# Gated-delta mixer of a two-layer hybrid block on one core: key and query norm sums as two float32r passes, and matrix steps dealt behind later value units

## The chip, the cores and the metric

The kernel runs on one core of a Trainium2 chip. The metric is the device time of one execution in microseconds (us); a time "of a kernel" is the median of several executions.

## The reference

The block has two layers on x of 512 tokens by 1024 features, all in float32. A layer normalises x, multiplies it by one wide matrix `w_in`, runs four mixers (a: gated delta rule, b: dilated window attention, c: stick-breaking attention, d: retention), multiplies each result by its branch matrix and a sigmoid gate, adds them, applies `w_o`, and follows with a two-matrix MLP. Cut to the part that the change touches:

```python
qkv = jax.nn.silu(causal_dwconv(gdn_qkv, conv_w))            # mixer a
qa, ka, va = split(qkv)
qa = l2norm(to_heads(qa, 4)) * 128 ** -0.5                   # x * rsqrt(sum(x*x) + 1e-6), 128 features a head
ka = l2norm(to_heads(ka, 4))
g = -exp(a_log) * softplus(gdn_a + dt_bias)                  # per token and head
oa = gated_delta_chunked(qa, ka, va, sigmoid(gdn_b), g)
#   per chunk: decay = exp(cumsum differences of g);  lower = (k*beta) k^T * decay below the diagonal
#   t_inv = (I + lower)^-1;  attn = q k^T * decay;  a scan over chunks with a 128x128 state a head
```

## The kernel before

**Engines and data.** Tensors lie feature-major: 128 features on the partitions, 512 tokens in a row. SP loads the weights in 182 units a layer of 256 rows by 512 columns; POOL splits each into a rounded float32r part (L579) and the rest (L581), in a ring of four; PE multiplies in three float32r passes, high by high, low by high, high by low (`unit`, L1744): 24 products of 512 columns for a unit of two 128-row tiles and four output tiles, so 12 for half a unit (two output tiles). The order on every engine is written out by hand in `tensor_layer`, `vector_layer`, `scalar_layer`; engines meet through counting semaphores.

**PSUM.** There are eight banks: `big0` to `big3` take the outputs of weight units, `mix0` to `mix3` everything else, in the order of the list `mixer_keys()`, each key in the next bank. A bank's next user on PE waits for `big_free`/`mix_free` of its last. The four output tiles of `av` (values) stand in big1, big2, big3, big0, and those of the next job, `gatea0`, in the same four. An `av` bank is given back by `conv_raw(i)` on ACT (i = 8 to 11): it copies the tile to a mix bank (L719) and then, scaled, to SBUF (L720), whose end frees the big bank. The mix banks of raw 8 to 11 are those of LT0, att0, LT1, att1, so `conv_raw(8)` also waits until DVE is through with LT0.

**The stage of the change (mixer a).** On PE: `aq` (queries), `ak` (keys), `aab`, then the four units of `av`. Behind them are dealt, by `value_unit(i)`:

- `l2_sums`: for each of the 4 query and 4 key head tiles, the sum of squares over the 128 partitions, as one float32 product of a matrix of ones with the squares `q_sq` (L1855);
- `gates_by_token` (four small transposes), `gc` (cumulative sums of g), `gt` (its rows);
- `decays(b)`: rows R and B of token block b, broadcast over partitions; `lower(b)` the matrix LT(b); `scores_gdn(b)` the matrix att(b).

ACT makes the squares (`qk_squares`, L731) and the roots (`qk_root`, L736, L738); DVE scales with them (`qk_normed`, L1292). After `decays`, ACT computes exponentials for blocks 0 and 1 (`row_exponents`), copies LT0 (`lower_copy`, L785), then runs `conv_raw(8)`, `conv_raw(9)`, `lower_copy(1)`, `conv_raw(10)`, `conv_raw(11)`. DVE runs for each block `beta_keys`, `lower`, `scores_out`, `first_level` (its last instruction, L1357, frees LT's bank), `first_inverse` (L1363), and only behind both blocks the convolutions 8 to 11 (`conv`, L1284 twice and L1286 each), which free the four mix banks for the products Y and X of the first level of the triangular inverse: Y of blocks 0 and 1 take the banks of raw 8 and 9, X those of raw 10 and 11. Both layers run the same program; layer 1 repeats layer 0's stage 1144.77 us later.

The order of PE in this stage is these lines (L1929 to L1946):

```python
unit(JOB["av"], 2, (0, 1)); value_unit(2); unit(JOB["av"], 2, (2, 3))
decays(0); decays(1)
unit(JOB["av"], 3, (0, 1))
lower(0); scores_gdn(0)                    # after waits for the l2 banks
unit(JOB["av"], 3, (2, 3))
lower(1); scores_gdn(1)
set_fill("gatea0", "az")                   # fills[0], fills[1]: units 0 and 1 of gatea0
for tiles in ((0, 1), (2, 3)):
    for q in range(2): unit(*fills[q], tiles)
```

Of the kernel before, what the change touches and what calls it, by code (L numbers as in the profile page):

```python
# [278 lines left out]

EIGHTHS = (("Y", 1), ("X", 1), ("Y", 2), ("Y", 3), ("Y", 4), ("X", 4), ("Y", 5), ("Y", 6))  # L280


def mixer_keys():
# [51 lines left out]
    "a_silu": 12, "a_small": 2, "a_smallact": 4, "a_sq": 8, "a_tap": 24, "a_z": 4, "a_zero": 1, "an_rs": 4,  # L335
    "an_sq": 4, "b_exp": 36, "b_fc": 3, "b_fexp": 3, "b_max": 12, "b_nm": 12, "b_ohi": 5, "b_olo": 5, "b_rhi": 9,
    "b_rlo": 9, "b_rp": 9, "b_share": 2, "b_sum": 3, "b_zinv": 1, "b_zln": 1, "big_done0": 43, "big_done1": 43,
    "big_done2": 38, "big_done3": 38, "big_free0": 43, "big_free1": 43, "big_free2": 38, "big_free3": 38,
    "c_act": 40, "c_add": 8, "c_bias": 3, "c_exp": 20, "c_half": 4, "c_hi": 8, "c_ln": 20, "c_ohi": 4, "c_pos": 20,
    "c_pv": 4, "c_pvfree": 4, "c_split": 8, "c_sum": 20, "c_z": 20, "d_nrm": 4, "d_ohi": 4, "d_olo": 4, "d_out": 4,  # L340
    "d_rope": 4, "d_rp": 4, "dn_rs": 4, "dn_sq": 4, "f_hi": 32, "f_lo": 32, "f_relu": 32, "gated_b": 8,
# [7 lines left out]
    "w_loaded3": 720, "w_ready": 182, "w_used": 182, "x_hi": 8, "x_lo": 8, "x_ss": 3, "x_ss1": 1,  # L349
# [3 lines left out]
def hybrid_kernel(nc, ins, out):  # L353
    ctx = ExitStack()
    with ctx:
# [229 lines left out]
        def scalar_layer(act, l):  # L585
# [97 lines left out]
            def gate_sigmoid(b):  # L683
                for hf in range(2):
                    if b == "c":
                        for i in range(2):
                            big_freed(act, (f"gatec{2 * hf + 1}", i))
                    else:
                        big_freed(act, (f"gate{b}{hf}", 3))
                    A(gate_at(b, hf), gate_at(b, hf), ACT.Sigmoid).then_inc(sem(f"sig{b}"), 1)  # L690
# [36 lines left out]
            def qk_squares(i):  # L727
                if i >= 4:
                    mix_wait(act, ("l2", i - 4))
                act.wait_ge(*upto("a_silu", i + 1))  # L730
                A(q_sq[:, i % 4, :], (aQ, aK)[i // 4][:, i % 4, :], ACT.Square).then_inc(sem("a_sq"), 1)  # L731
# [379 lines left out]
        def vector_layer(dve, l):  # L1111
# [87 lines left out]
            def gated_last():  # L1199

                def last_lo(k):
                    key = (f"yb{k // 4}", k % 4)
                    dve.wait_ge(*upto("m_hi", k + 1))
                    big_free(TT(hL[:, k, :], home(key)[0][:, :], f32(hH[:, k, :]), ALU.subtract), key)

                for hf in range(2):
                    for k in range(4 * hf, 4 * hf + 4):
                        ps = big_wait(dve, (f"yb{k // 4}", k % 4))
                        dve.wait_ge(*upto("sigb", k // 4 + 1))
                        TT(ps[:, :], ps[:, :], sg[:, k, :], ALU.mult).then_inc(sem("gated_b"), 1)  # L1210
                        dve.wait_ge(*upto("gated_b", k + 1))
                        TT(ps[:, :], ps[:, :], mixed[:, k, :], ALU.add).then_inc(sem("mixed_b"), 1)
                        if k % 4:
                            last_lo(k - 1)
                    last_lo(4 * hf + 3)

            def gated(b):

                for hf in range(2):
                    for i in range(4):  # L1220
                        k = 4 * hf + i
                        ps = big_wait(dve, (f"y{b}{hf}", i))
# [483 lines left out]
        def tensor_layer(pe, l):  # L1706
# [162 lines left out]
            def value_unit(i):  # L1869
                if i == 0:  # L1870
                    l2_sums(0, 1, 2, 3)
                if i == 1:
                    gates_by_token()
                    l2_sums(4, 5, 6, 7)
# [3 lines left out]
                if i == 2:  # L1878
# [539 lines left out]
```

## Time and profile before

| | |
|---|---|
| time of three runs | 2310.89, 2307.17, 2311.28 us; median 2310.89 |
| profiled execution | 2309.96 us, of it span 2308.2 us |
| PE (matmul) busy | 2282.2 us, 99% of the span |
| DVE, ACT, POOL busy | 862.5 (37%), 739.5 (32%), 1281.5 us (56%) |
| granted TensorE clock | 0.996 mean |

The profile is of one execution. "Busy" of PE is modelled, since matmuls are pipelined: a product of 512 columns is listed with 0.39 us, and the next starts 0.23 us after it. For PE's pace read the distance of starts. Start times are counted from the start of the span.

### The profile page before, as it was taken

How to read it: one execution, taken by the hardware profiler on the slowest of the kernel's cores; microseconds unless marked ns; L12 is line 12 of the kernel's file. 1: busy time of each engine (PE TensorE's matmuls, PEld its weight loads, DVE VectorE, ACT ScalarE, POOL GpSimd, SP SyncE). 2: the span in 40 equal slices, each digit the busy share in tenths (PEclk: the TensorE clock that was granted, in tenths of full speed). 3: DMA queues.
4: the chain of work that ended last, by engine and by line, in shares of the span. 5: the costliest groups of instructions: out<-in, count | busy, mean ns of one | idle time of the engine just before them, and what ended most of it. 6: DMA issues, size and time to landing. Idle time of an engine off the chain costs nothing.

```text
span 2308.2 us, 30524 instructions
## 1 busy us (share of the span) xinstructions
PE 2282.2 (99%) x12414; PEld 1848.9 (80%) x12414; DVE 862.5 (37%) x1390; ACT 739.5 (32%) x1465; POOL 1281.5 (56%) x732
## 2 busy tenths in 40 slices
PE   8999999999999999999999999999999999999998
PEld 7788877877877788888887888778778768888887
DVE  4654025424354421122355540444234545112233
ACT  5633145123044411122355340461220545102121
POOL 5523644555553566677655146546556445666874
PEclk9999999999999999999999999999999999999999
DMA  4311321423222233332223123223233123333231
GB/s 152 92 47 47 100 73 55 119 82 91 74 78 61 91 119 100 92 100 92 83 79 92 29 65 101 65 82 96 77 94 90 60 69 104 103 96 101 92 101 64
DMA packets 105899, 196.64 MB, mean 85 GB/s; under 512 B 8480, under 2 KB 18848, under 8 KB 105504
## 3 DMA queue, kind: packets, MB, share of 16 engines
q1 hardware_dynamic: 104608, 188.40, 27.1%
q10 hardware_dynamic: 1152, 6.29, 0.8%
q8 instruction: 99, 1.62, 0.3%
q14 instruction: 40, 0.33, 0.0%
HBM read 192.57 MB, written 2.10 MB: 84 GB/s over the span
## 4 chain that ended last, share of the span: by engine, by line
PE 95%; ACT 2%; DVE 2%; issue 1%; DMA 0%; DVEq 0%; ACTq 0%
PE big L1744 72%; PE mix L1744 10%; PE mix L1895 4%; PE big L2097 1%; PE mix L2065 1%; PE mix L2167 1%; PE mix L2076 1%; PE mix L1855 1%; PE mix L2295 1%; PE mix L2248 0%; PE mix L1809 0%; ACT o_hi L616 0%; PE mix L2232 0%; PE mix L2218 0%; PE mix L2024 0%
## 5 line engine op out<-in xcount | busy, mean ns | idle before, releaser
L581 POOL TENSOR_TENSOR ring_lo<-stage,ring_hi 128x1024 fp32r<-128x1024 f32 (+3 forms) x364 | 911.6, 2504 | 30.4
L579 POOL TENSOR_SCALAR ring_hi<-stage 128x1024 fp32r<-128x1024 f32 (+3 forms) x364 | 371.4, 1020 | 972.7 <-PE big L1744 892.1
L1744 PE MATMUL big<-h_hi,ring_hi 128*128 128x512 f32 (+1 forms) x1888 | 721.5, 382 | 2.9 <-DVE h_lo L1166 1.7
L1744 PE MATMUL big<-h_lo,ring_hi 128*128 128x512 f32 (+1 forms) x1888 | 708.6, 375 | 0.0
L1744 PE MATMUL big<-h_hi,ring_lo 128*128 128x512 f32 (+1 forms) x1888 | 708.5, 375 | 0.0
L1744 PEld LDWEIGHTS big<-h_hi,ring_hi 128*128 128x128 f32 x1888 | 354.7, 188 | 74.9 <-issue 8.9
L1744 PEld LDWEIGHTS big<-h_lo,ring_hi 128*128 128x128 f32 x1888 | 354.7, 188 | 66.0
L1744 PEld LDWEIGHTS big<-h_hi,ring_lo 128*128 128x128 f32 x1888 | 355.0, 188 | 62.0 <-issue 1.4
L1685 DVE TENSOR_TENSOR h_lo<-scr,h_hi 128x1024 fp32r<-128x1024 f32 x64 | 86.8, 1356 | 246.4 <-ACT h_hi L1084 246.4
L1744 PE MATMUL big<-ring_hi,h_hi 128*128 128x512 f32 x448 | 174.2, 390 | 0.0
L1744 PE MATMUL big<-ring_lo,h_hi 128*128 128x512 f32 x448 | 174.1, 390 | 0.0
L1744 PE MATMUL big<-ring_hi,h_lo 128*128 128x512 f32 x448 | 173.7, 389 | 0.0
L1084 ACT ACTIVATE h_hi<-scr 128x1024 fp32r<-128x1024 f32 x64 | 68.4, 1069 | 262.2 <-PE big L1744 260.2
L1696 DVE SCALAR_TENSOR_TENSOR scr<-big,scr 128x512 f32<-128x512 f32 x64 | 44.3, 692 | 254.5 <-ACT scr L1093 254.3
L1744 PE MATMUL mix<-ring_hi,h_hi 128*128 128x512 f32 x320 | 125.0, 391 | 0.0
L1744 PE MATMUL mix<-ring_hi,h_lo 128*128 128x512 f32 x320 | 124.6, 389 | 0.0
L1744 PE MATMUL mix<-ring_lo,h_hi 128*128 128x512 f32 x320 | 124.5, 389 | 0.0
L1093 ACT ACTIVATE scr<-big 128x512 f32<-128x512 f32 x64 | 38.3, 598 | 262.1 <-PE big L1744 261.2
L1744 PEld LDWEIGHTS big<-ring_hi,h_hi 128*128 128x128 f32 x448 | 84.1, 188 | 18.1 <-issue 0.7
L1744 PEld LDWEIGHTS big<-ring_lo,h_hi 128*128 128x128 f32 x448 | 83.8, 188 | 18.2 <-POOL ring_lo L581 1.0
L1744 PEld LDWEIGHTS big<-ring_hi,h_lo 128*128 128x128 f32 x448 | 84.1, 188 | 17.6
L1744 PE MATMUL big<-o_hi,ring_hi 128*128 128x512 f32 x224 | 90.4, 403 | 1.0 <-ACT scr L674 0.9
(302 smaller groups left out, 2717.4 us busy)
## 6 DMA issues: line engine op xcount, KB each, us to landing
stage<-in_w_in SPq DMA_DIRECT2D x168, 512.0 KB, 3.5
stage<-in_w_mlp_in SPq DMA_DIRECT2D x64, 512.0 KB, 3.6
stage<-in_w_mlp_out SPq DMA_DIRECT2D x64, 512.0 KB, 3.8
stage<-in_w_o SPq DMA_DIRECT2D x16, 512.0 KB, 3.8
stage<-in_w_br_a SPq DMA_DIRECT2D x8, 512.0 KB, 3.8
stage<-in_w_br_c SPq DMA_DIRECT2D x8, 512.0 KB, 3.8
stage<-in_w_br_d SPq DMA_DIRECT2D x8, 512.0 KB, 3.8
stage<-in_w_br_b SPq DMA_DIRECT2D x8, 512.0 KB, 3.6
```

The lines of the kernel that those rows point to most:

```text
L579: nc.gpsimd.tensor_scalar(rH[jw][0:pp, r, 0:kk, 0:job.n], w, 1.0, 0.0, ALU.mult, ALU.add).then_inc(sem("w_hi"), 1)
L581: nc.gpsimd.tensor_tensor(rL[jw][0:pp, r, 0:kk, 0:job.n], w, f32(rH[jw][0:pp, r, 0:kk, 0:job.n]), ALU.subtract).then_inc(sem("w_ready"), 1)
L1084: A(hH[:, q:q + 2, :], fT[:, 2 * u:2 * u + 2, :], ACT.Copy).then_inc(sem("f_hi"), 1)
L1093: A(fT[:, 4 * g + i, :], ps[:, :], ACT.Relu).then_inc(sem("f_relu"), 1)
L1685: TT(hL[:, q:q + 2, :], fT[:, 2 * u:2 * u + 2, :], f32(hH[:, q:q + 2, :]), ALU.subtract).then_inc(sem("f_lo"), 1)
L1696: big_free(STT(fT[:, k, :], ps[:, :], 0.0, fT[:, k, :], ALU.max, ALU.mult), (f"up{g}", i))
L1744: ins_ = MM(o_, a_, r_, start=s0, stop=s1)
L1855: done(MM(ps[:, :], f32(ones_r[:, 0:1]).to_broadcast((P, P)), q_sq[:, i % 4, :], start=True, stop=True), ("l2", i))
L1895: return MM(o_, a_, b_, start=True, stop=True)
L2065: i = MM(c_bank[u][:, at:at + w], hv(cK, h)[:, j * P:(j + 1) * P], hv(cQ, h)[:, j * P:], start=opens, stop=True, skip_group_check=True)
L2076: MM(c_bank[u][:, :], rot_r[:, 2 * P:3 * P], part[:, u, :], start=False, stop=True, skip_group_check=True)
L2097: r = MM(c_out[e * DH:e * DH + DH, j * P:], cV[:, j, (2 * p + e) * DH:(2 * p + e + 1) * DH], c_A[:, u, at:at + S - j * P], start=j == 0, s ...
```

## The change

- `qk_squares` (ACT) writes the square of a query tile twice: in float32 to `q_sq`, and rounded to float32r to `oH`. For a key tile it writes only the rounded one.
- DVE gets two new steps. `square_lo(i)` subtracts the rounded square from the float32 one and writes the rest to `oL` (8 a layer); for the keys DVE makes the float32 square itself (`TT ... mult` on aK, 4 a layer). `square_lo` of the queries stands between the convolutions 3 and 4; those of the keys alternate with `qk_normed(0..3)`.
- `l2_sums` (PE) makes each sum in two float32r passes, ones by `oH` and ones by `oL`.
- The sums of keys 4 and 5 stay behind av's unit 1; those of 6 and 7, with `gc`, move behind the first half of unit 2; `gt` moves from there to behind all of unit 2.
- `decays(0)` and `decays(1)` move behind the first half of unit 3; `lower(0)` and `scores_gdn(0)` behind its second half; `lower(1)` and `scores_gdn(1)` behind the first half of gatea0's unit 0. Three halves of gatea0 follow before the inverse, where four stood.
- The semaphores `siga` to `sigd` become one, `sig`, and `gated_b`, `gated_c`, `gated_d` one, `gated`, with offsets; the waits mean the same.

```diff
 def qk_squares(i):                                   # ACT
     ...
-    A(q_sq[:, i % 4, :], (aQ, aK)[i // 4][:, i % 4, :], ACT.Square).then_inc(sem("a_sq"), 1)
+    x = (aQ, aK)[i // 4][:, i % 4, :]
+    if i < 4:
+        A(q_sq[:, i, :], x, ACT.Square)
+    A(oH[:, i % 4, :], x, ACT.Square).then_inc(sem("a_sq"), 1)

-for i in range(8):                                   # DVE
+def square_lo(i):
+    dve.wait_ge(*upto("a_sq", i + 1))
+    if i >= 4:
+        dve.wait_ge(*upto("a_sqk", i - 3))
+    TT(oL[:, i % 4, :], q_sq[:, i % 4, :], f32(oH[:, i % 4, :]), ALU.subtract).then_inc(sem("a_sqlo"), 1)
+
+for i in range(4):
     conv(i)
 for i in range(4):
+    square_lo(i)
+for i in range(4, 8):
+    conv(i)
+for i in range(4):
+    dve.wait_ge(*upto("a_silu", i + 5))
+    dve.wait_ge(*upto("a_sqlo", i + 1))
+    TT(q_sq[:, i, :], aK[:, i, :], aK[:, i, :], ALU.mult).then_inc(sem("a_sqk"), 1)
+for i in range(4):
+    square_lo(i + 4)
     qk_normed(i)

 def l2_sums(*tiles):                                 # PE
     for i in tiles:
         ps = tile_of(("l2", i))
-        pe.wait_ge(*upto("a_sq", i + 1))
-        done(MM(ps[:, :], f32(ones_r[:, 0:1]).to_broadcast((P, P)), q_sq[:, i % 4, :], start=True, stop=True), ("l2", i))
+        pe.wait_ge(*upto("a_sqlo", i + 1))
+        ones = ones_r[:, 0:1].to_broadcast((P, P))
+        MM(ps[:, :], ones, oH[:, i % 4, :], start=True, stop=False)
+        done(MM(ps[:, :], ones, oL[:, i % 4, :], start=False, stop=True), ("l2", i))

 def value_unit(i):                                   # PE
     ...
     if i == 1:
         gates_by_token()
-        l2_sums(4, 5, 6, 7)
+        l2_sums(4, 5)
+    if i == 2:
+        l2_sums(6, 7)
         pe.wait_ge(*upto("a_g", 2))
         ...                                          # gc
-    if i == 2:
+    if i == 3:
         mix_freed(pe, "gc")
         ...                                          # gt

 unit(JOB["av"], 2, (2, 3))
+value_unit(3)
+unit(JOB["av"], 3, (0, 1))
 decays(0)
 decays(1)
-unit(JOB["av"], 3, (0, 1))
+unit(JOB["av"], 3, (2, 3))
+set_fill("gatea0", "az")
 for i in range(4, 8):
     mix_freed(pe, ("l2", i))
 lower(0)
 scores_gdn(0)
-unit(JOB["av"], 3, (2, 3))
+unit(*fills[0], (0, 1))
 lower(1)
 scores_gdn(1)
-set_fill("gatea0", "az")
-for tiles in ((0, 1), (2, 3)):
-    for q in range(2):
-        unit(*fills[q], tiles)
+unit(*fills[1], (0, 1))
+for q in range(2):
+    unit(*fills[q], (2, 3))
```

**Where PE's instructions stand.** First place, PE, layer 0, from the gate transposes to the next value unit: `mix1<-scr,ones_r` is the sum of one head tile in mix bank 1, `128x16` is gc, `16x128` gt, `big..<-h_hi,ring_hi` the first product of an output tile of av. Before:

```order
L1861 MATMUL mix0<-consts,scr 128x8 [waits a_ab,mix_free0]
...
L1855 MATMUL mix1<-scr,ones_r 128x512 [waits a_sq,mix_free1]
L1855 MATMUL mix2<-scr,ones_r 128x512 [waits a_sq,mix_free2]
L1855 MATMUL mix3<-scr,ones_r 128x512 [waits a_sq,mix_free3]
L1855 MATMUL mix0<-scr,ones_r 128x512 [waits a_sq,mix_free0]
L1877 MATMUL mix1<-st,consts 128x16 [waits mix_free1,a_g]
L1744 MATMUL big1<-h_hi,ring_hi 128x512 [waits w_ready]
...
L1895 MATMUL mix2<-consts,st 16x128 [waits mix_free2,mix_free1]
```

With the change:

```order
L1884 MATMUL mix0<-consts,scr 128x8 [waits a_ab,mix_free0]
...
L1877 MATMUL mix1<-o_hi,ones_r 128x512 [waits a_sqlo,mix_free1]
L1878 MATMUL mix1<-o_lo,ones_r 128x512
L1877 MATMUL mix2<-o_hi,ones_r 128x512 [waits a_sqlo,mix_free2]
L1878 MATMUL mix2<-o_lo,ones_r 128x512
L1765 MATMUL big1<-h_hi,ring_hi 128x512 [waits w_ready]
...
L1877 MATMUL mix3<-o_hi,ones_r 128x512 [waits a_sqlo,mix_free3]
L1878 MATMUL mix3<-o_lo,ones_r 128x512
L1877 MATMUL mix0<-o_hi,ones_r 128x512 [waits a_sqlo,mix_free0]
L1878 MATMUL mix0<-o_lo,ones_r 128x512
L1902 MATMUL mix1<-st,consts 128x16 [waits mix_free1,a_g]
L1765 MATMUL big3<-h_hi,ring_hi 128x512 [waits w_ready]
```

Each sum has become two instructions, two of the key sums and gc stand half a value unit later, and gt has left this stretch.

Second place, PE, layer 0, around the two matrix steps: `64x64` rows are LT(b), `128x128` rows att(b), big1 and big2 the first two output tiles. Before:

```order
L1895 MATMUL mix3<-scr 64x64 [waits mix_free0,mix_free3,mix_free2,mix_free1]
...
L1895 MATMUL mix0<-scr 128x128 [waits mix_free0]
...
L1744 MATMUL big3<-h_hi,ring_hi 128x512 [waits w_ready]
...
L1895 MATMUL mix1<-scr 64x64 [waits mix_free1,mix_free2]
...
L1895 MATMUL mix2<-scr 128x128 [waits mix_free2]
...
L1744 MATMUL big1<-h_hi,ring_hi 128x512 [waits big_free1,w_ready]
...
L1744 MATMUL big2<-h_hi,ring_hi 128x512 [waits big_free2]
```

With the change:

```order
L1920 MATMUL mix3<-scr 64x64 [waits mix_free0,mix_free3,mix_free2,mix_free1]
...
L1920 MATMUL mix0<-scr 128x128 [waits mix_free0]
...
L1765 MATMUL big1<-h_hi,ring_hi 128x512 [waits big_free1,w_ready]
...
L1765 MATMUL big2<-h_hi,ring_hi 128x512 [waits big_free2]
...
L1920 MATMUL mix1<-scr 64x64 [waits mix_free1,mix_free2]
...
L1920 MATMUL mix2<-scr 128x128 [waits mix_free2]
...
L1765 MATMUL big1<-h_hi,ring_hi 128x512 [waits w_ready]
```

The first products of gatea0, which wait for `big_free1` and `big_free2`, stood behind LT(1) and att(1); now they stand between att(0) and LT(1).

Third place, ACT, the instructions that free those banks (in both kernels the same rows; these are of the changed one, where L791, L722, L723 are the L785, L719, L720 of before):

```order
L791 ACTIVATE scr<-mix3 128x256 [waits a_LTm0]
L722 ACTIVATE mix3<-big1 128x512 [waits mix_free3,big_done1]
L723 ACTIVATE scr<-big1,lw 128x512
L722 ACTIVATE mix0<-big2 128x512 [waits mix_free0,big_done2]
L723 ACTIVATE scr<-big2,lw 128x512
L791 ACTIVATE scr<-mix1 128x256 [waits a_LTm1]
L722 ACTIVATE mix1<-big3 128x512 [waits mix_free1,big_done3]
L723 ACTIVATE scr<-big3,lw 128x512
L722 ACTIVATE mix2<-big0 128x512 [waits mix_free2,big_done0]
```

`big1` is free when the first L723 ends, and the L722 ahead of it waits for `mix_free3`, the bank of LT(0). Nothing moved here.

## Rows read from the trace of the kernel before

**Rows 1.** The page: engines' busy time, and the chain that ended last, by engine.

```profile
PE 2282.2 (99%) x12414; PEld 1848.9 (80%) x12414; DVE 862.5 (37%) x1390; ACT 739.5 (32%) x1465; POOL 1281.5 (56%) x732
...
PE 95%; ACT 2%; DVE 2%; issue 1%; DMA 0%; DVEq 0%; ACTq 0%
```

**Rows 2.** PE's waits: waited for; us in total, times, longest us.

```profile
PE big L1809 <- ACT scr L631: 10.2, 4, 8.9
PE big L1744 <- DVE h_lo L1166: 1.7, 2, 1.5
```

**Rows 3.** Timeline, PE, query sums, layer 0: start, duration, instruction, count.

```profile
72.64 3.59 PE L1855 MATMUL mix<-scr,ones_r 128*128 128x512 f32 x8
75.67 0.80 PE L1744 MATMUL big<-h_hi,ring_hi 128*128 128x512 f32 x1
76.31 0.39 PE L1744 MATMUL big<-h_hi,ring_lo 128*128 128x512 f32 x1
```

**Rows 4.** Timeline, PE, a sum in two float32r passes, in mixer d.

```profile
513.52 0.40 PE L2033 MATMUL mix<-o_hi,ones_r 128*128 128x512 f32 x1
513.75 0.40 PE L2034 MATMUL mix<-o_lo,ones_r 128*128 128x512 f32 x1
513.99 1.67 PE L2167 MATMUL mix<-scr 128*128 128x512 f32 x4
```

**Rows 5.** Timeline, PE, layer 0: LT and att of blocks 0 and 1.

```profile
95.58 2.23 PE L1895 MATMUL mix<-scr 128*64 128x64 f32 x32
97.56 0.48 PE L1744 MATMUL big<-h_hi,ring_hi 128*128 128x512 f32 x1
...
100.49 2.23 PE L1895 MATMUL mix<-scr 128*64 128x64 f32 x32
```

**Rows 6.** Timeline, ACT, layer 0: `conv_raw` 8 and 10; in brackets the idle time before.

```profile
100.16 0.58 ACT L719 ACTIVATE mix<-big 128x512 f32<-128x512 f32 x1 [1.29 <-DVE g_uc L1357]
100.65 0.68 ACT L720 ACTIVATE scr<-big,lw 128x512 f32<-128x512 f32 x1
...
105.57 0.68 ACT L720 ACTIVATE scr<-big,lw 128x512 f32<-128x512 f32 x1
```

**Rows 7.** Timeline, DVE, layer 0: last convolution instruction, and the work after it.

```profile
113.66 0.75 DVE L1286 SCALAR_TENSOR_TENSOR scr<-mix,lw,scr 128x509 f32<-128x509 f32 x1
114.33 1.12 DVE L1238 TENSOR_TENSOR scr<-scr,consts 128x256 f32<-128x256 f32 x2
```

**Rows 8.** Timeline, PE, layer 0: products Y and X of the first level.

```profile
113.56 1.12 PE L1895 MATMUL mix<-scr 64*64 64x32 f32 x32
...
115.51 1.12 PE L1895 MATMUL mix<-scr,g_uc 64*64 64x32 f32 x32
```

**Rows 9.** Timeline, PE, mixer b of both layers: 3-row products, and the first after them.

```profile
723.18 6.19 PE L2295 MATMUL mix<-scr,consts 3*128 3x512 f32 x14
729.30 0.80 PE L1744 MATMUL big<-o_hi,ring_hi 128*128 128x512 f32 x1
...
1867.91 7.36 PE L2295 MATMUL mix<-scr,consts 3*128 3x512 f32 x14
1875.20 0.80 PE L1744 MATMUL big<-o_hi,ring_hi 128*128 128x512 f32 x1
```

**Rows 10.** Windows: PE, PEld, DVE, ACT, POOL busy, then the granted clock (PEclk), DMA.

```profile
727.00:733.00 6.00, 6.00 (x12) 3.26 (x11) 4.68 (x7) 4.10 (x5) 2.65 (x2) 0.50 0.00 0
...
1870.00:1880.00 10.00, 10.00 (x21) 4.98 (x18) 6.51 (x9) 6.26 (x8) 3.76 (x2) 0.50 0.01 2
```

**Rows 11.** Timeline, layer 0, DVE and PE between the sums and gt.

```profile
75.46 0.69 DVE L1292 SCALAR_TENSOR_TENSOR scr<-scr,mix 128x512 f32<-128x512 f32 x1 [7.61 <-ACT mix L738]
...
88.31 0.17 DVE L1316 COPY st<-mix 128x16 f32<-128x16 f32 x1
...
88.58 0.40 PE L1895 MATMUL mix<-consts,st 128*16 128x128 f32 x4
```

**Rows 12.** Groups by shape, DVE: busy us, mean ns | idle before.

```profile
L1527 DVE TENSOR_TENSOR o_lo<-scr,o_hi 128x512 fp32r<-128x512 f32 x16 | 23.3, 1454 | 90.4 <-ACT o_hi L832 90.2
```

More of the change, by code:

```diff
@@ L278 @@
 LEVELS = 7
+SIG_AT = {"a": 0, "c": 2, "d": 4, "b": 6}
+GATED_AT = {"c": 0, "d": 8, "b": 16}
 EIGHTHS = (("Y", 1), ("X", 1), ("Y", 2), ("Y", 3), ("Y", 4), ("X", 4), ("Y", 5), ("Y", 6))
@@ L334 @@
     "a_nrm": 4, "a_ohi": 4, "a_olo": 4, "a_one": 2, "a_out": 4, "a_qd": 4, "a_rhi": 2, "a_rs": 8, "a_sc": 3,
[L335 to L341, printed above, removed]
[1 row of a table removed]
+    "a_silu": 12, "a_small": 2, "a_smallact": 4, "a_sq": 8, "a_sqk": 4, "a_sqlo": 8, "a_tap": 24, "a_z": 4,
+    "a_zero": 1, "an_rs": 4, "an_sq": 4, "b_exp": 36, "b_fc": 3, "b_fexp": 3, "b_max": 12, "b_nm": 12, "b_ohi": 5,
+    "b_olo": 5, "b_rhi": 9, "b_rlo": 9, "b_rp": 9, "b_share": 2, "b_sum": 3, "b_zinv": 1, "b_zln": 1,
+    "big_done0": 43, "big_done1": 43, "big_done2": 38, "big_done3": 38, "big_free0": 43, "big_free1": 43,
+    "big_free2": 38, "big_free3": 38, "c_act": 40, "c_add": 8, "c_bias": 3, "c_exp": 20, "c_half": 4, "c_hi": 8,
+    "c_ln": 20, "c_ohi": 4, "c_pos": 20, "c_pv": 4, "c_pvfree": 4, "c_split": 8, "c_sum": 20, "c_z": 20, "d_nrm": 4,
+    "d_ohi": 4, "d_olo": 4, "d_out": 4, "d_rope": 4, "d_rp": 4, "dn_rs": 4, "dn_sq": 4, "f_hi": 32, "f_lo": 32,
[1 row of a table added]
     "mix_free0": 58, "mix_free1": 57, "mix_free2": 57, "mix_free3": 57, "mixed_b": 8, "n2_half": 4, "n2_ln": 4,
@@ L346 @@
     "pre1_lo": 24, "pre1_nw": 8, "pre1_v": 4, "pre1_y": 4, "pre2_h": 8, "pre2_half": 4, "pre2_hi": 32, "pre2_ln": 4,
[2 rows of a table removed]
-    "w_loaded3": 720, "w_ready": 182, "w_used": 182, "x_hi": 8, "x_lo": 8, "x_ss": 3, "x_ss1": 1,
[2 rows of a table added]
+    "w_used": 182, "x_hi": 8, "x_lo": 8, "x_ss": 3, "x_ss1": 1,
 }
@@ L689, in gate_sigmoid @@
                         big_freed(act, (f"gate{b}{hf}", 3))
-                    A(gate_at(b, hf), gate_at(b, hf), ACT.Sigmoid).then_inc(sem(f"sig{b}"), 1)
+                    A(gate_at(b, hf), gate_at(b, hf), ACT.Sigmoid).then_inc(sem("sig"), 1)
             if l == 0:
@@ L1208, in gated_last @@
                         ps = big_wait(dve, (f"yb{k // 4}", k % 4))
-                        dve.wait_ge(*upto("sigb", k // 4 + 1))
-                        TT(ps[:, :], ps[:, :], sg[:, k, :], ALU.mult).then_inc(sem("gated_b"), 1)
-                        dve.wait_ge(*upto("gated_b", k + 1))
+                        dve.wait_ge(*upto("sig", SIG_AT["b"] + k // 4 + 1))
+                        TT(ps[:, :], ps[:, :], sg[:, k, :], ALU.mult).then_inc(sem("gated"), 1)
+                        dve.wait_ge(*upto("gated", GATED_AT["b"] + k + 1))
                         TT(ps[:, :], ps[:, :], mixed[:, k, :], ALU.add).then_inc(sem("mixed_b"), 1)
@@ L1222, in gated @@
                         ps = big_wait(dve, (f"y{b}{hf}", i))
-                        dve.wait_ge(*upto(f"sig{b}", hf + 1))
+                        dve.wait_ge(*upto("sig", SIG_AT[b] + hf + 1))
                         if b == "a":
@@ L1226, in gated @@
                         else:
-                            TT(ps[:, :], ps[:, :], sg[:, k, :], ALU.mult).then_inc(sem(f"gated_{b}"), 1)
-                            dve.wait_ge(*upto(f"gated_{b}", k + 1))
+                            TT(ps[:, :], ps[:, :], sg[:, k, :], ALU.mult).then_inc(sem("gated"), 1)
+                            dve.wait_ge(*upto("gated", GATED_AT[b] + k + 1))
                             big_free(TT(mixed[:, k, :], ps[:, :], mixed[:, k, :], ALU.add), (f"y{b}{hf}", i))
```

6 rows, old and new, of the table PER_LAYER are left out of this document.

## The prediction

> **What bounds the kernel now.** I read the page first: PE is busy for 99% of the span and makes 95% of the chain that ended last, while DVE, ACT and POOL are busy for 56% or less [rows 1]. Then PE's waits: the largest is at the start of the program, and the next holds 1.7 us in total [rows 2]. So the time is the sum of what PE issues, and a change can gain only by taking work off PE, and can lose by making PE wait where it does not wait today. Everything else I read from timelines of layer 0, by the distance of starts, and double it, since layer 1 repeats the stage. A difference under 0.2% (4.6 us) can't be told from no change here.
>
> **The sums.** Four float32 sums start at 72.64, and the second product behind them at 76.31; one product takes 0.23, so the four took 76.31 - 0.23 - 72.64 = 3.44 us, 0.86 each [rows 3]. In the changed form a sum is two float32r passes. Mixer d has exactly such pairs, with the same matrix of ones: 513.52 to 513.99, 0.47 a pair [rows 4]. Eight sums a layer save 8 x 0.39 = 3.1 us, both layers 6.2 us.
>
> **What feeds them.** ACT makes four more squares (a pass of this size takes it 0.58 us [rows 6]) and DVE eight subtractions and four multiplications a layer. A subtraction into `oL` has a row with 1.45 us [rows 12], other DVE passes of this size take 0.69 [rows 11]; so 12 of them cost DVE 8 to 17 us a layer. For the queries they fall while `ak` is multiplied; for the keys the multiplications fall into the 7.61 us in which DVE waited before its first scaling [rows 11], and the subtractions alternate with the scalings, between which DVE waits for ACT's roots. At 0.69 all of it is hidden. The place with little cover is gt: today the copy of gc starts on DVE at 88.31 and PE issues gt at 88.58 [rows 11]. The change puts gt half a unit (2.7 us) further back in the order, and everything before it runs 3.1 earlier, so gt comes at about 88.2; the sums of keys 6 and 7 end at about 84.9 and two roots and two scalings behind them put the copy at about 87.6. I cost this at nothing; with the slower subtraction it would be about 1 us a layer.
>
> **The moved steps.** `decays` moves half a unit back and the sums give the same amount back, so `lower(0)` starts about 0.4 us earlier than its 95.58. What matters is what follows it. Call the start of `lower(0)` S0. LT(0) and att(0) take 97.56 - 95.58 = 1.98 us [rows 5]. Today half a unit of av follows, which needs no bank. With the change the first half of gatea0 follows, and its first product waits for `big_free1` (the second and third order pieces): the bank of value tile 0, which `conv_raw(8)` on ACT gives back. That ACT step waits for DVE to be through with LT(0) (it idled 1.29 us until DVE's last instruction on it), starts at 100.16, and its second instruction ends at 100.65 + 0.68 = 101.33 [rows 6]. That is S0 + 5.75, and the chain from LT(0) over DVE's and ACT's work to it does not depend on anything PE issues later, so it keeps this distance. PE arrives at S0 + 1.98. So **PE waits 3.8 us, and with the restart 3.95 us (0.2 is my estimate: a first product after a switch is listed with 0.48 instead of 0.39 us [rows 3, 5], and I take twice the difference), where it does not wait today**. The second output tile is free 1.1 us after the first and the first takes 1.4 us, so it adds nothing.
>
> **Behind it.** `lower(1)` starts after that half unit, at S0 + 5.95 + 2.8; call it S1. Today S1 is 100.49. From LT(1), DVE goes through block 1 and then the convolutions 8 to 11; the last ends at 113.66 + 0.75 = 114.41, S1 + 13.9 [rows 5, 7]. The second X product takes the bank of convolution 11. Today it starts in the middle of the X row, at 115.51 + 0.53 = 116.04, S1 + 15.55 [rows 8], so it has 1.6 us to spare. One half unit (2.72 us) has moved from behind LT(1) to before it, so PE now gets there at S1 + 12.83 and **waits another 1.15 us** (most of it already at the third tile of gatea0, whose bank ACT frees at 105.57 + 0.68 = 106.25 [rows 6], S1 + 5.76, when PE gets there at S1 + 4.8; both waits overlap in this sum). Behind it the levels keep their distances: DVE still finishes its masks and subtractions before PE's next level wants them.
>
> A layer: -3.1 + 3.95 + 1.15 = +2.0. Both: +4.0 us.
>
> **The clock.** The trace shows what a stretch with little work does to TensorE: in mixer b, after 6.19 and 7.36 us of products with 3 rows [rows 9], the granted clock is 0.50, the 1.2 GHz level, from 727 to 733 and from 1870 to 1880 [rows 10], so it stayed down for about 4 us after full products had resumed at 729.30 and at 1875.20. No row shows a wait of 4 us in mid-program. The cost of the half rate after one lies between nothing and 2.2 us a layer (4 to 4.9 us at half rate, half of it lost). I take 1.5: nearer the upper end, because a wait is even emptier than 3-row products, but it is shorter than both stretches. Both layers: +3.0 us.
> The Trainium skill, page "TensorE: Matmul & The Clock Gate", part 1 (the HAM clock gate), says that the half rate is the default state and that only activity releases the full one, so a pause between bursts brings the half rate back. The rows agree with it; by it alone the sum would hold this term, and without it the result is the first rival below.
>
> **The sum.** +4.0 + 3.0 = +7.0 us against the profiled execution's 2309.96: 2317.0 us. The median of the runs is 0.9 us above that execution, so the median would be 2317.9; the profiled time lies inside the runs' spread of 4.1 us, and I predict 2317.5.
>
> **The rivals.**
> *No loss at the clock.* The waits come as worked out, but the clock stays at 1.00 in and behind them. For it: the clock did not fall at any other place of this stage, small products of 64 rows [rows 8] among them, and the wait is shorter than the low stretches of mixer b. Against it: rows 9 and 10. Time: 2310.9 + 4.0 = 2314.9, within 0.2% of no change. Chance 0.25.
> *Faster: the bank is free in time.* One mechanism decides the sign: when `conv_raw(8)` ends after the start of `lower(0)`. If PE got to gatea0 later, or ACT freed the bank, within 1.98 us of S0, the first wait would be gone. The second remains, since DVE's convolutions don't move: -3.1 + 1.15 = -1.95 a layer, -3.9, 2307.0; with it hidden too, -6.2, 2304.7. The point from which it decides: the first wait must be under 2 us a layer for the time to fall below today's. For it speaks only that I read the chain from one execution; against it that the wait is worked out as twice that, and that layer 1 has the same distances. Chance 0.1.
> *The feeding is late.* The subtractions on DVE run at 1.45 us, as the same operation does in mixer d [rows 12]; gc's copy comes late, and PE waits about 1 us more a layer at gt or at the key sums, on top of the forecast: 2319 to 2322. The row of 1.45 speaks for it, the idle time of DVE at this place against it. Chance 0.08.
> That the change doesn't do what it says is excluded by the order of instructions: the sums are pairs, and the steps stand where the text puts them.
>
> **How the numbers follow.** The forecast, both waits and a clock loss, has a chance of 0.57. Its own range is 2314 to 2321: the clock term may be 0 to 4.4 us in all, and the length of the half rate in mixer b (6 us in one layer, 10 in the other) may come out differently when the program shifts, which is worth up to 2 us either way. For 8 in 10 I add the first rival, down to 2311, and leave out the fast one and the upper end beyond 2322. Slower by over 0.2% means above 2315.5: nearly all of the forecast, with the late feeding, 0.62. Within 0.2%: the first rival, what the forecast leaves below 2315.5, and half of the fast one, 0.30. Faster by over 0.2%, below 2306.3: 0.08.
>
> **What would show it.** PE's waits must list a new one before the products of the first gatea0 tile, released by ACT's scaled copy of `conv_raw(8)`, 3.5 to 4 us, once a layer, and PE's busy time must fall by it. LT(1) should start about 8.7 us after LT(0), not 4.9. The sums must stand 0.47 us apart. A wait of about 1 us a layer should stand at the third tile of gatea0 or at X, released by ACT or DVE. PEclk should show 0.50 for some us around or right behind the long wait, with products 0.43 us apart there. The prediction is wrong if PE runs through from LT(0) to LT(1) in under 6 us, or if the sums don't get cheaper; and its clock term is wrong if PEclk stays at 1.00 after the wait.

## The result: slower by 2%, and the profile after

The changed kernel takes 2357.86 us (median of four runs, 2355.91 to 2359.94), the kernel before 2311.05 (four runs on the same chip). The ratio is 1.0206, with a 95% interval from 1.019 to 1.0222. The forecast was slower, at 2317.5 us: 6.5 us of loss, where there are 46.8.

The page of the changed kernel, where [rows 1] stood: busy time and the chain by engine.

```profile
PE 2313.8 (98%) x12414; PEld 1881.2 (80%) x12414; DVE 903.4 (38%) x1414; ACT 743.7 (32%) x1473; POOL 1287.8 (55%) x732
...
PE 92%; DVE 4%; ACT 2%; issue 2%; DMA 0%; DVEq 0%; ACTq 0%
```

PE is busy for 31.6 us longer (2313.8 - 2282.2), with as many instructions and with sums that cost less: it works, but slowly. The mean granted clock is 0.979, where it was 0.996.

PE's waits, where [rows 2] stood (waited for; us in total, times, longest us):

```profile
PE big L1765 <- ACT scr L723: 9.2, 4, 3.7
PE mix L1902 <- DVE scr L1298: 4.4, 2, 2.2
PE mix L1920 <- issue: 3.7, 2, 1.9
...
PE mix L1877 <- DVE scr L1298: 1.4, 2, 0.7
```

Four kinds of wait are new, 18.7 us in all for two layers. The timeline of PE in layer 0 shows where they stand and how the sums came out (where [rows 3, 5, 8] stood):

```profile
73.53 0.40 PE L1877 MATMUL mix<-o_hi,ones_r 128*128 128x512 f32 x1
73.76 0.40 PE L1878 MATMUL mix<-o_lo,ones_r 128*128 128x512 f32 x1
74.00 0.39 PE L1877 MATMUL mix<-o_hi,ones_r 128*128 128x512 f32 x1
...
89.49 0.58 PE L1902 MATMUL mix<-st,consts 128*128 128x16 f32 x2 [2.21 <-DVE scr L1298]
...
101.18 2.23 PE L1920 MATMUL mix<-scr 128*64 128x64 f32 x32
107.08 0.77 PE L1765 MATMUL big<-h_hi,ring_hi 128*128 128x512 f32 x1 [3.67 <-ACT scr L723]
112.47 2.59 PE L1920 MATMUL mix<-scr 128*64 128x64 f32 x32
118.73 0.47 PE L1765 MATMUL big<-h_hi,ring_hi 128*128 128x512 f32 x1 [0.91 <-ACT scr L723]
124.37 1.12 PE L1920 MATMUL mix<-scr 64*64 64x32 f32 x32
126.32 1.14 PE L1920 MATMUL mix<-scr,g_uc 64*64 64x32 f32 x32
130.20 1.82 PE L1920 MATMUL mix<-scr 64*64 64x32 f32 x32 [1.86 <-issue]
```

The sums stand 0.47 apart. The wait for cumulative gates (2.21), the bank wait (3.67) with a second one (0.91) on a later tile, and the wait at 130.20 (1.86), ahead of Y of the second level, are the new ones. The last is put down to "issue", but DVE tells who it is. DVE and then POOL in the same stretch, where [rows 7] stood:

```profile
126.00 0.75 DVE L1292 SCALAR_TENSOR_TENSOR scr<-mix,lw,scr 128x509 f32<-128x509 f32 x1
126.66 3.24 DVE L1244 TENSOR_TENSOR scr<-scr,consts 128x256 f32<-128x256 f32 x2
129.82 0.47 DVE L1445 TENSOR_TENSOR scr<-scr,mix 128x128 f32<-128x128 f32 x2
```

```profile
126.08 1.04 POOL L582 TENSOR_SCALAR ring_hi<-stage 128x1024 fp32r<-128x1024 f32 x1 [0.47 <-PE big L1765]
127.21 2.40 POOL L584 TENSOR_TENSOR ring_lo<-stage,ring_hi 128x1024 fp32r<-128x1024 f32 x1
```

The two level masks (L1244, the L1238 of before) take 3.24 us, where they took 1.12 [rows 7]. Both inputs of a mask lie in SBUF, and the second mask ends at 129.90, 0.3 us after POOL's subtraction (127.21 + 2.40 = 129.61). Behind it, DVE takes X out of its bank at 129.82, and PE goes on at 130.20.

Windows of PE busy, loads, DVE, ACT, POOL, then the granted clock, DMA; in the kernel before, all of these stretches read 1.00:

```profile
90.00:95.00 5.00, 5.00 (x19) 3.63 (x19) 1.74 (x4) 1.08 (x3) 0.00 (x0) 0.72 0.24 88
105.00:110.00 5.00, 2.92 (x7) 2.37 (x8) 1.08 (x3) 2.26 (x4) 1.90 (x2) 0.65 0.01 2
110.00:115.00 5.00, 5.00 (x39) 3.89 (x39) 0.99 (x3) 0.00 (x0) 1.50 (x1) 0.67 0.36 105
130.00:135.00 5.00, 4.80 (x63) 4.02 (x65) 2.11 (x7) 1.07 (x3) 0.00 (x0) 0.54 0.39 108
135.00:160.00 25.00, 25.00 (x286) 20.77 (x283) 8.89 (x25) 5.11 (x13) 0.00 (x0) 0.50 0.01 2
...
1304.00:1334.00 30.00, 30.00 (x323) 25.43 (x323) 10.89 (x29) 5.11 (x13) 0.00 (x0) 0.50 0.01 2
```

There are three stretches at 0.50 (1.2 GHz) in each layer: about 3.4 us behind the gates' wait, 6.8 behind the bank wait, and **34 us behind the wait of 1.86 us**, from 130.4 to 164.5 and in layer 1 from 1301 to 1335. In the last one PE is busy throughout. The balance of the two profiled spans, 2358.1 - 2308.2 = 49.9 us: waits +18.7, sums -6.2, which leaves 37.4 for the half rate. The clock says the same: twice 1 - 0.979 makes 4.2% of the span at half rate (99 us), before 0.8% (18 us), so 81 us more, of which half is lost, 40 us; the three stretches of both layers are 88 us.

### The profile page after: what moved, and what is told of

Its sections match the earlier page's. It is cut to its first block, busy times and chain, and to the rows that moved or that the text cites. A ratio compares the mean times of both kernels' runs of the same rounds, so it can differ in the third digit from the quotient of the medians.

```text
span 2358.1 us, 30572 instructions
## 1 busy us (share of the span) xinstructions
PE 2313.8 (98%) x12414; PEld 1881.2 (80%) x12414; DVE 903.4 (38%) x1414; ACT 743.7 (32%) x1473; POOL 1287.8 (55%) x732
## 4 chain that ended last, share of the span: by engine, by line
PE 92%; DVE 4%; ACT 2%; issue 2%; DMA 0%; DVEq 0%; ACTq 0%
PE big L1765 69%; PE mix L1765 9%; PE mix L1920 5%; PE big L2124 1%; PE mix L2092 1%; PE mix L2194 1%; PE mix L2103 1%; DVE scr L1290 1%; PE mix L2275 0%; PE mix L2322 0%; DVE o_lo L1304 0%; DVE scr L1315 0%; PE mix L1830 0%; ACT o_hi L619 0%; PE mix L2259 0%
## 5 line engine op out<-in xcount | busy, mean ns | idle before, releaser
L1765 PE MATMUL big<-h_hi,ring_hi 128*128 128x512 f32 (+1 forms) x1888 | 729.5, 386 | 11.9 <-ACT scr L723 9.2
L1765 PE MATMUL big<-h_hi,ring_lo 128*128 128x512 f32 (+1 forms) x1888 | 716.1, 379 | 0.0
L1765 PEld LDWEIGHTS big<-h_hi,ring_lo 128*128 128x128 f32 x1888 | 359.8, 191 | 61.8 <-issue 1.0
L1920 PEld LDWEIGHTS mix<-scr 64*64 64x64 f32 (+2 forms) x1216 | 79.3, 173 | 15.9 <-issue 13.4
```

The lines of the kernel that those rows point to most:

```text
L1765: ins_ = MM(o_, a_, r_, start=s0, stop=s1)
L1920: return MM(o_, a_, b_, start=True, stop=True)
```

## The experiments

Three explanations stood. **Theory 1: short waits start it and the half clock costs**, above all the 34 us behind the masks' wait. **Rivals**: the two-pass sums with their feed cost it; or the bank wait of the new order does. Times below stand beside the kernel before on the same chip (medians 2307.3 to 2309.5 us), and where a kernel is compared with the changed one, it is the loss of each against its own kernel before that is compared (46.8 us for the changed one).

**The sums alone** (PE's order as before, the rest as changed):

```diff
 if i == 1:
     gates_by_token()
-    l2_sums(4, 5)
+    l2_sums(4, 5, 6, 7)                  # gc right behind, gt, decays, lower as before
```

> The two-pass sums with all that feeds them, and TensorE's order as it was before the change. Theory 1 (three short waits that the change makes, and the half clock that follows them, above all the 34 us at half clock in each layer's inverse levels): the bank wait at the first gate half and the late level masks belong to the new order, so both go; what stays is the late feed, whose wait now lies where all four key sums stand in a row: 2 to 5 us a layer plus 1.5 to 3 us of half clock, less 3.1 for the sums. 2308 to 2322 us, clock about 0.995, and 1.00 in the inverse levels. Rival 2 (the sums with their feed cost it themselves, wherever they stand): about the changed kernel's 2350 to 2360. Rival 3 (the new order costs it through the bank wait alone): 2305, the full gain of the sums.

Measured: 2318.7 us, ratio 1.0043 (1.0027 to 1.0060), clock 0.992. PE's waits name what is left:

```profile
PE mix L1877 <- DVE scr L1298: 5.5, 4, 2.0
PE mix L1900 <- DVE scr L1298: 1.8, 2, 0.9
```

The sums with their feed cost 9 us instead of gaining 6.2: 3.7 us of waits a layer, and about 6.8 us a layer at 0.50 behind them. The inverse levels read 1.00. So the feed is not free, but it is not the 47 us.

**The order alone** (one float32 sum over one square, PE's order as changed):

```diff
-    l2_sums(4, 5, 6, 7)                  # in the kernel before
+    l2_sums(4, 5)                        # 6, 7 and gc, gt, decays, lower where the change puts them
```

> TensorE's new order alone (key sums behind two value units, decays and first lower matrix behind the last one), with the sums as one float32 pass over one square. Theory 1: the bank wait at the first gate half stays (3 to 4 us a layer, and about 6 us at half clock behind it, 3 us lost), the wait on the late feed goes, DVE has 8 multiplications and 8 subtractions less ahead of the conv rows but that work is over by then, so the level masks still meet GpSimd's splits: the third wait and the 34 us at half clock stay if the masks fall at the same place. 2340 to 2358 us if it stays, 2325 if the stretch keeps its clock. Rival 2 (the sums with their feed cost it): near 2311. My prediction's own terms (waits, and 1.5 us of clock a layer): 2324.

Measured: 2348.6 us, but its four runs are 2338.5, 2341.7, 2355.5 and 2355.5; ratio 1.0170 (1.0133 to 1.0207). The profiled execution is one of the short ones, and its two layers show why. PE ahead of the second level's Y, in layer 0 and layer 1:

```profile
128.07 1.92 PE L1897 MATMUL mix<-scr 64*64 64x32 f32 x32 [1.87 <-issue]
```

```profile
1295.67 1.12 PE L1897 MATMUL mix<-scr 64*64 64x32 f32 x32 [1.85 <-issue]
```

The windows behind them:

```profile
135.00:160.00 25.00, 25.00 (x257) 20.78 (x254) 8.99 (x23) 4.84 (x12) 0.00 (x0) 0.50 0.01 2
...
1300.00:1334.00 34.00, 33.98 (x418) 29.36 (x418) 18.91 (x46) 14.76 (x38) 6.88 (x4) 1.00 0.08 20
```

It is the same wait with the same 32 products behind it. In layer 0 they take 1.92 us and the clock reads 0.50 for the 25 us from 135; in layer 1 they take 1.12, and 1300 to 1334 reads 1.00. One kept stretch is worth some 15 us, the distance between the pairs of runs. (Only one of the four has a trace; that the long ones lost the clock in both layers is read from their mean clock, 0.981 against 0.987 and 0.989.) The new order without the new sums makes most of the loss, and does so through the clock.

**POOL held back while DVE does the masks:**

```diff
 ...                                                 # POOL, between L582 and L584 of each unit u
+if u == UNIT_AT["az", 1]:
+    b_, k_ = MIX["X", 1, 1]                         # DVE has taken X of the first level
+    pool.wait_ge(*upto(f"mix_free{b_}", k_))
```

> The changed kernel, but GpSimd holds the split of the gate's next weight until VectorE has taken the X matrix of the first level out of its bank. So no split runs while VectorE does the level masks. Theory 1: the masks take 1.1 us again instead of 3.2, the wait of 1.9 us ahead of the small products goes or is under 0.5 us, and the clock stays at 1.00 through the inverse levels: 17 us less a layer, 2320 to 2330 us, clock near 0.99. Rival (the half clock of the inverse levels comes from what the bank wait did to the clock 20 us earlier, not from the wait at the masks): the clock is 0.50 there all the same, 2352 to 2358.

Measured: 2324.3 us, ratio 1.0069 (1.0054 to 1.0084): a loss of 14.8 us, 32 less than that of the changed kernel, for one wait on an engine that is busy 55% of the time. DVE, PE, and the window of the levels:

```profile
122.92 1.09 DVE L1247 TENSOR_TENSOR scr<-scr,consts 128x256 f32<-128x256 f32 x2
...
125.24 2.31 DVE L1247 TENSOR_TENSOR scr<-scr,consts 128x256 f32<-128x256 f32 x2
```

```profile
124.54 1.12 PE L1923 MATMUL mix<-scr 64*64 64x32 f32 x32
...
127.85 1.12 PE L1923 MATMUL mix<-scr 64*64 64x32 f32 x32 [0.25 <-issue]
```

```profile
135.00:160.00 25.00, 24.98 (x274) 22.08 (x270) 13.48 (x30) 13.03 (x33) 5.37 (x4) 1.00 0.08 23
```

The masks take 1.09 us, the wait ahead of the second level's Y is 0.25 us, and the levels run at 1.00, although the bank wait of 3.7 us and the gates' wait of 2.2 stand where they stood. (The held subtraction now falls on the next level's masks, which take 2.31 us; that wait of 0.25 us is all that comes of it.) So the two earlier waits do not bring the long stretch on by themselves. They did less to the clock in this execution, though: it stayed at 1.00 behind the gates' wait and read 0.50 for 3.4 us behind the bank wait, where the changed kernel had 3.4 and 6.8. Whether the long stretch needs them at all is left to the delay alone, below.

**No gate half between the lower matrices:**

```diff
-unit(*fills[0], (0, 1))
 lower(1)
 scores_gdn(1)
-unit(*fills[1], (0, 1))
-for q in range(2):
-    unit(*fills[q], (2, 3))
+for tiles in ((0, 1), (2, 3)):
+    for q in range(2):
+        unit(*fills[q], tiles)
```

> The changed kernel without a gate half between the two lower matrices: all four halves of the gate stand behind the second one, as before the change. Theory 1: the wait of 3.7 us on the bank and its 6.8 us at half clock go; the second lower matrix comes about 6 us earlier, so VectorE is through its conv rows about 6 us earlier too and the masks meet GpSimd's splits at another place. 14 us in two layers less at least: 2344, and about 2325 if the wait at the masks falls under 1 us and the inverse levels keep the clock. Rival (the late feed, which stays here, is what brings the half clock of the levels on): 2350 or more, with 0.50 in the levels.

Measured: 2314.1 us, ratio 1.002 (1.001 to 1.003): a loss of 6.5 us, 40 less than that of the changed kernel and better than I expected. The bank wait is 1.5 us instead of 3.67, and no 0.50 stands behind it. The masks start at 119.69 and take 0.97 us: they now fall between two of POOL's subtractions, one that ends at 120.05 and one that starts at 121.65. The levels read 1.00, although the late feed is all there, so the rival of the expectation falls too. So the placing of one half unit decides both, the bank wait itself and whether the masks meet POOL.

**A delay alone, in the kernel before.** First with many small memsets ahead of the masks:

```diff
 mix_wait(dve, ("Y", b, n - 1))
+if (b, n) == (0, 2):
+    for r in range(20):                             # 32 in the second run
+        V.memset(g_vb[:, r // 8, 16 * (r % 8):16 * (r % 8) + 16], 0.0)
```

> The kernel before the change, with 20 small memsets of dead space on VectorE ahead of the level masks of the first level, in each layer: nothing else moves. They delay VectorE by about 1.9 us (0.09 each) and should make TensorE wait 1.1 us more ahead of the second level's small products (the row of VectorE before had 0.8 us in hand). Theory 1 (a wait at this place is enough for the half clock, whatever came earlier): a wait near the 1.9 us of the changed kernel, summed with what stands there, gives 34 us at half clock in some layers of some runs: 2312 if it does not fall, 2329 with one layer, 2346 with both. Rival (the wait alone costs only itself; the clock falls because of earlier waits): 2310 to 2313, clock 0.996.

> As the run with 20 memsets, with 32: 3 us of delay on VectorE, about 2.2 us more wait at the same place in each layer. Theory 1: the clock falls in both layers and stays at half through the inverse levels: 2309 + 4.5 + 2 x 17 = 2347 us, clock 0.98. Rival (the wait costs only itself): 2314, clock 0.996.

Measured: 2309.2 and 2308.6 us, both ratios 1.000. This test missed: 31 memsets took 0.79 us, 25 ns each and not 90, and that is what the masks had in hand. It shows only that a delay inside the 0.8 us costs nothing. Then with large ones, each waiting for the one ahead:

```diff
+    for r in range(3):                              # under the same condition; 4 and 6 in the other runs
+        V.memset(g_vb, 0.0).then_inc(sem("a_dly"), 1)
+        dve.wait_ge(*upto("a_dly", r + 1))
```

> The kernel before the change, with three memsets of a dead 128x512 tile in a row on VectorE ahead of the level masks of the first level, each waiting for the one ahead; nothing else moves. The two runs with 20 and 32 small memsets had set out to do this and missed: 32 took 0.8 us in all, which the 0.8 us in hand hid. A 64x256 memset takes 0.28 us, so 128x512 should take about 0.55 with its wait 0.65: 1.9 us of delay, about 1.1 us of wait on TensorE. Theory 1 (a wait at this place is enough for the half clock): below the 1.9 us of the changed kernel, so it may hold: 2310 if it holds, 2327 with one layer, 2344 with both. Rival (the wait costs only itself): 2310, clock 0.996.

> As the run with three large memsets, with four: 2.6 us of delay, about 1.8 us of wait in each layer, as much as in the changed kernel. Theory 1: 2328 with one layer at half clock, 2345 with both, more or less by chance from run to run. Rival (the half clock needs the waits that the changed kernel has 7 and 17 us earlier): 2311.5, clock 0.996.

> As the run with four large memsets, with six: 3.9 us of delay, about 3 us of wait in each layer. Theory 1: both layers at half clock through the inverse levels in all executions, 2309 + 6 + 34 = about 2349 us, clock 0.98. Rival: 2315, clock 0.996.

Measured: 2342.1 us (ratio 1.0140, 1.0124 to 1.0157), 2340.8 (1.0137, 1.0122 to 1.0152) and 2340.5 (1.0135, 1.0118 to 1.0151). With six memsets one of the four executions took 5927.68 us, for a cause that nothing here shows; it is the profiled one, so no line is read from it, and the interval rests on the other three (2338.6 to 2340.9). DVE, PE, and windows (PE busy, clock, DMA) with three memsets:

```profile
115.84 0.48 DVE L1240 MEMSET scr<- 128x512 f32 x1
...
117.68 2.92 DVE L1242 TENSOR_TENSOR scr<-scr,consts 128x256 f32<-128x256 f32 x2
```

```profile
120.90 1.92 PE L1899 MATMUL mix<-scr 64*64 64x32 f32 x32 [2.00 <-issue]
```

```profile
130.00:150.00 20.00, 20.00 (x231) 0.50 0.01 2
...
155.00:160.00 5.00, 5.00 (x46) 1.00 0.10 12
```

The delay of 1.8 us pushed the masks into POOL's subtraction (117.79 to 120.32), where they took 2.92 us. PE waited 2.00 us, in both layers, and the clock read 0.50 until about 154.8, some 34 us. **Two waits of 2.0 us, with no other new wait in PE's list and the clock at 1.00 up to them, cost the kernel before 34.8 us.** With four memsets the waits are 2.16 us and the cost is the same, and there the profile names what PE waited for, which it put down to "issue" before: DVE's subtraction of X (L1428, the L1445 of the changed kernel).

```profile
PE mix L1899 <- DVE scr L1428: 4.3, 2, 2.2
```

The rival's 2310 to 2315 is far off. In all eight executions with three and four memsets the mean clock is 0.982 to 0.984 and the time 2337 us or more, where a layer that kept its clock would leave about 2327: it fell in both layers each time. Six memsets were to give 3 us of wait and 2349 us, and gave no more than three. With no trace of it I can only estimate why: a memset with its wait takes 0.66 us, so six put the masks at about 119.8, and POOL's subtraction, which set their end with three and four, was about to end by then; the wait would hardly have grown.

**Towards a version that beats both.** ACT makes both squares of the keys right behind their silu, in buffers of their own, so that DVE multiplies nothing; PE's order is that of before:

```diff
-    if i < 4:
-        A(q_sq[:, i, :], x, ACT.Square)
-    A(oH[:, i % 4, :], x, ACT.Square).then_inc(sem("a_sq"), 1)
+    A(q_sq[:, i % 4, :], x, ACT.Square)
+    A((oH, c_H)[i // 4][:, i % 4, :], x, ACT.Square).then_inc(sem("a_sq"), 1)
```

> TensorE's order of before, two-pass sums, but ScalarE makes both squares of the keys right behind their silu into buffers of their own, so that VectorE multiplies nothing and GpSimd's splits block only its subtractions. Theory 1: the feed is early enough for most of the key sums: 2305 to 2312 us, clock 0.995 to 0.996, no half clock in the inverse levels. Rival (VectorE's subtractions alone are blocked long enough by GpSimd): a wait of 1 to 3 us a layer is left, with half clock behind it, 2311 to 2318.

Measured: 2312.6 us, ratio 1.0013 (1.0004 to 1.0022). The key sums run without a wait, and gc waits 2.6 us a layer, since it needs the bank of the first key sum. The clock stayed at 1.00 behind it in both layers of the profiled execution. DVE's subtractions are still blocked: 2.03 us each.

The same, with gc and gt half a unit later and decays behind the first half of unit 3 (no gate half between the lower matrices):

```diff
 unit(JOB["av"], 2, (2, 3))
+value_unit(3)                            # gt; gc stands behind the first half of unit 2
+unit(JOB["av"], 3, (0, 1))
 decays(0)
 decays(1)
-unit(JOB["av"], 3, (0, 1))
+unit(JOB["av"], 3, (2, 3))
 lower(0)
 scores_gdn(0)
-unit(JOB["av"], 3, (2, 3))
 lower(1)
```

> The fourth run's kernel (both squares of the keys by ScalarE, two-pass sums) with the cumulative gates one half of a value unit later, their transposes one half later and the decays behind the last unit's first half, and no gate half between the lower matrices. Theory 1: the 2.6 us wait of the fourth run goes; VectorE's chain of the second lower matrix starts up to 1.8 us later than before the change, of which about 1 us may show at the first level. 2304 to 2309 us, clock 0.996, if that wait is too short for the clock; 2315 to 2325 if it brings the half clock on in a layer.

Measured: 2307.2 us against 2307.7, ratio 0.9992 (0.9983 to 1.0002). gc no longer waits, but the gate's first tile waits 1.5 us for its bank: half a unit has gone from between LT(0) and it.

The same two squares by ACT, with the key sums half a unit earlier instead, so that nothing later needs to move:

```diff
-for i in range(2):
-    unit(JOB["av"], i)
-    value_unit(i)
+unit(JOB["av"], 0)
+value_unit(0)
+unit(JOB["av"], 1, (0, 1))
+value_unit(1)                            # gate transposes, the four key sums
+unit(JOB["av"], 1, (2, 3))
+value_unit(2)                            # gc; gt behind the first half of unit 2
 ...
```

> The kernel of the sixth run (both key squares by ScalarE) with the key sums moved half a value unit earlier, into the middle of the second unit, the cumulative gates behind that unit, and then TensorE's order of before the change, with a value half between the two lower matrices. The sums are ready by then (VectorE had the last one at 75.7 us in the fourth run, and the spot comes at 77.4), so neither the wait of 2.6 us (fourth run) nor the bank wait of 1.5 us (sixth run) should stand; 0.7 us a layer may, where the cumulative gates wait for VectorE's small chain. 6.2 - 1.4 = 4.8 us under the kernel before: 2303 us. If ScalarE's roots or VectorE's norms are later than that: 2306.

Measured: 2302.0 us against 2307.3, ratio 0.9973 (0.9963 to 0.9984). PE, the last sums, gc and LT(0):

```profile
80.13 0.40 PE L1871 MATMUL mix<-c_hi,ones_r 128*128 128x512 f32 x1
80.36 0.39 PE L1872 MATMUL mix<-c_lo,ones_r 128*128 128x512 f32 x1
83.36 0.29 PE L1895 MATMUL mix<-st,consts 128*128 128x16 f32 x2
...
93.41 2.23 PE L1913 MATMUL mix<-scr 128*64 128x64 f32 x32
```

LT(0) starts 2.2 us earlier than in [rows 5], no wait is left in the stage, and the levels run at 1.00. The part of the change that saves work was sound; with both key squares on ACT it is worth 5.3 us where it makes PE wait nowhere.

## Why the prediction was right in sign and wrong in size

- **The sums, -3.1 us a layer: right.** A pair takes 0.47, eight of them save what [rows 3, 4] gave.
- **The feeding, "I cost this at nothing": wrong.** I had priced DVE's 12 passes at 0.69 to 1.45 us. The 0.69 is that of a scaling, which has one input in PSUM, and the 1.45 is a mean over passes of 0.72 to 2.48 us, some of them beside POOL already; I took it for the price of a slow operation and placed gc's copy by order alone. In the trace of the changed kernel POOL splits weights back to back from 65.5 to 88.4, and DVE's passes with two SBUF inputs take far longer. DVE by line, in 60 to 90 us:

```profile
L1315 DVE TENSOR_TENSOR scr<-scr 128x512 f32<-128x512 f32 x4 | 7.9, 2025 | 0.0
L1304 DVE TENSOR_TENSOR o_lo<-scr,o_hi 128x512 fp32r<-128x512 f32 x4 | 7.0, 1752 | 0.0
...
L1298 DVE SCALAR_TENSOR_TENSOR scr<-scr,mix 128x512 f32<-128x512 f32 x6 | 3.9, 666 | 0.0
```

  Squares and subtractions take 2.03 and 1.75 us; the scaling of the same size, with one input in PSUM, takes 0.67. Waits of 0.72 us (the second key sum) and 2.21 us (gc) a layer came of it, and 3.4 us at half clock. The rival "the feeding is late" had the engine and roughly the place (it named gt and the key sums; gt does not wait), at a third of what the waits alone came to and a chance of 0.08. The Trainium skill, page "SBUF — State Buffer", section "SBUF: two separate sides", says of the port pair that VectorE and GpSimd share that one of them holds it and the other waits when VectorE takes two inputs from SBUF. The rows bear it out: the scalings, with one SBUF input, are not slowed beside the same POOL work.
- **The bank wait, 3.95 us a layer: right in place, releaser and size.** The list of waits has 3.67, once a layer, released by ACT's L723. By the distance of starts, as I had worked it out, LT(0) to the first product of the gate takes 107.08 - 101.18 = 5.90 us, where I had 5.95. LT(1) then starts 11.29 us after LT(0) and not 8.7, since the half unit between them runs at half rate.
- **The second wait, 1.15 us: the place was half right.** 0.91 us stands at the gate's third tile, as written.
- **"Behind it the levels keep their distances: DVE still finishes its masks and subtractions before PE's next level wants them": the step that failed most.** I had moved the masks in time by DVE's own chain, and did not ask what else runs there. Pushed from 114.33 to 126.66, they fell under POOL's subtraction, took 3.24 instead of 1.12 us, and PE waited 1.86 us ahead of the second level. Holding POOL back left 0.25 us of that wait, and took 32 us of the loss with it.
- **The clock, 1.5 us a layer: mis-sized by more than ten times** (about 20 us a layer). I bounded what a wait costs by the low stretches of mixer b [rows 9, 10], where full products follow at once and the rate is back in 4 to 5 us. Behind the bank wait such products follow as well, and 6.8 us at half rate (3.4 lost) came, above the 2.2 that I had as the upper end. But behind the wait at 130.20 come the inverse levels, small float32 products with a few full ones between, and there the half rate stayed for 34 us. That it is these products that keep it low is read from the stretches behind the different waits; no run put full products behind this wait. The rows of this case that would have told me to ask are those of Y and X [rows 8]: 1.12 us for 32 products at 1.00, with nothing said of what they do to a clock that has already fallen.
- **The rivals.** "No loss at the clock" had a chance of 0.25, and the mechanism that it left out is the one that cost most; only "Faster" (0.1) lies further off. No rival had a short wait ahead of the small products. The range ended at 2322. The sign did not hang on the long stretch: with POOL held back it is gone, and the kernel still loses 14.8 us.

Not tried: the changed kernel with POOL held and no gate half at once; their gains overlap, since both take the wait at the masks away.

## What to carry to other kernels

Price a wait by what PE does behind it, not by its length alone: behind waits of 2.2 to 3.7 us ahead of full 512-column products these kernels ran 0 to 7 us at half rate, and behind one of 1.9 to 2.2 us ahead of a long run of small products 31 to 34 us, nearly half of it lost, unless the clock held, as it did once at 1.85. When a change shifts DVE's work in time, look up what POOL does at the new place: the two masks, with two SBUF inputs each, ended with POOL's subtraction there and took 2.1 us longer. And when a saving is real but what feeds it comes late, move the feeder and its user earlier, rather than users further back, where they meet the next bank.

## What the runs showed of the hardware beyond that

**The low clock can keep itself.** In the traces here the inverse levels run at 1.00 when they are entered at 1.00 and at 0.50 when the clock falls at their second level's Y, with the same instructions. Where the rate comes back in the changed kernel, PE has done float32 products of 128 rows and 128 to 256 columns for 4.3 us and begun on full ones:

```profile
162.40 1.20 PE L1920 MATMUL mix<-g_rows,rot_r 128*128 128x256 f32 x4
163.40 0.63 PE L1765 MATMUL big<-h_hi,ring_hi 128*128 128x512 f32 x1
...
164.60 0.40 PE L1765 MATMUL big<-h_hi,ring_hi 128*128 128x512 f32 x1
```

Starts are 0.43 us apart, then 0.24. With four memsets it came back at about 152.2, before the full products (from 153.13) had begun, after 31 us.

**Whether the clock falls at a wait of about 2 us is not settled by its length.** Ahead of the small products, with the new order alone, it stayed at 1.00 at 1.85 us in one layer and fell at 1.87 in the other, in one execution; it fell at 2.00 and 2.16 us in both layers of the two executions profiled with large memsets. The gates' wait of 2.2 us brought it down in both layers of the changed kernel and in neither with POOL held back, and gc's 2.6 us, in the kernel with early key squares, left it at 1.00 in both layers of the profiled execution (its other executions, mean clock 0.994 to 0.996, are up to 4.4 us longer).

**POOL pays too.** Its subtraction takes 2.71 us instead of 2.41 where DVE's two-input passes run against it. A pass of 16 columns with two SBUF inputs took 1.68 us on DVE, from 86.74 to 88.42, where the same pass took 0.18 in the kernel before (L1307, at 83.30, with POOL idle):

```profile
86.74 1.68 DVE L1328 TENSOR_TENSOR st<-st 128x16 f32<-128x16 f32 x1 [0.59 <-ACT st L768]
```

```profile
86.02 2.37 POOL L584 TENSOR_TENSOR ring_lo<-stage,ring_hi 128x1024 fp32r<-128x1024 f32 x1
```

The two end together: what the pass cost was the rest of POOL's instruction, not its own size. It stands in gc's way, too: behind it, at 88.72, comes the scaling of the first key, which frees the bank that gc waits for until 89.49.
